# Two weight subtractions put behind the first norm factor in GpSimd's queue

## The reference, cut to what matters

```
o_na = neighbourhood_attention(q_na, k_na, v_na, na_rpb)
o_mla = latent_attention(c_q, c_kv, k_rope, ...)
mixed = concatenate([rms_norm(o_na, na_out_norm_g),
                     rms_norm(o_mla, mla_out_norm_g)]) @ w_out
h = h + rms_norm(mixed, mix_post_g)
```

## Time and profile before

| | us |
|---|---|
| median of 3 runs | 953.36 |
| lowest and highest run | 953.24, 953.84 |
| the profiled execution's own time | 953.24 |
| its span in the profile | 951.5 |

### The profile page before, as it was taken

How to read it: one execution, slowest core, us unless ns; L and a number is a source line. 1 busy time by engine, 2 the same in 40 slices (tenths; PEclk the granted TensorE clock), 3 DMA queues, 4 the chain that set the end, 5 groups by cost and what they waited for, 6 DMA issues and landing times.

```text
span 951.5 us, 14116 instructions
## 1 busy us (share of the span) xinstructions
PE 938.2 (99%) x4854; PEld 788.5 (83%) x4854; DVE 506.2 (53%) x843; ACT 488.9 (51%) x782; POOL 283.1 (30%) x141
## 2 busy tenths in 40 slices
PE   8999999999999999999999999999999999999997
PEld 7999977778888888888888888888889878888886
DVE  5858967755653434523744343356477764433323
ACT  5577456653455444444644454447355664544441
POOL 1000000000044444444344444654441044444442
PEclk9999999999999999999999999999999999999999
DMA  7755566345555556787665655655512345666562
GB/s 245 242 173 167 178 216 193 113 153 197 176 162 191 183 191 189 269 230 206 188 189 179 190 187 188 220 154 166 173 61 92 111 155 180 188 187 193 179 195 71
DMA packets 132773, 169.36 MB, mean 178 GB/s; under 512 B 16708, under 2 KB 88431, under 8 KB 132599
## 3 DMA queue, kind: packets, MB, share of 16 engines
q1 hardware_dynamic: 132566, 168.67, 55.9%
q10 hardware_dynamic: 160, 0.07, 0.0%
HBM read 167.61 MB, written 1.10 MB: 177 GB/s over the span
## 4 chain that ended last, share of the span: by engine, by line
PE 95%; DVE 2%; ACT 2%; issue 1%; POOL 0%; DVEq 0%; POOLq 0%; ACTq 0%
PE acc L852 26%; PE acc L854 25%; PE acc L853 25%; PE tp L928 4%; PE acc L910 3%; PE acc L914 3%; PE acc L912 3%; PE acc L1194 1%; PE sc L1153 1%; PE sc L1003 1%; PE tp L1022 1%; DVE w_lo L1269 1%; ACT w_hi L506 0%; ACT junk L518 0%; PE sc L946 0%
## 5 line engine op out<-in xcount | busy, mean ns | idle before, releaser
L506 ACT ACTIVATE w_hi<-w_raw 128x1024 fp32r<-128x1024 f32 x301 | 318.3, 1059 | 363.9 <-PE acc L854 318.7
L1896 POOL TENSOR_TENSOR w_lo<-w_raw,w_hi 128x1024 fp32r<-128x1024 f32 x106 | 257.1, 2425 | 554.8 <-ACT w_hi L506 554.8
L1269 DVE TENSOR_TENSOR w_lo<-w_raw,w_hi 128x1024 fp32r<-128x1024 f32 x195 | 247.6, 1273 | 278.7 <-ACT w_hi L506 278.0
L852 PE MATMUL acc<-w_hi,xt_hi 128*128 128x512 f32 x704 | 279.7, 397 | 0.6 <-DVE w_lo L1269 0.3
L854 PE MATMUL acc<-w_lo,xt_hi 128*128 128x512 f32 x704 | 274.5, 390 | 0.0
L853 PE MATMUL acc<-w_hi,xt_lo 128*128 128x512 f32 x704 | 274.1, 389 | 0.0
L852 PEld LDWEIGHTS acc<-w_hi,xt_hi 128*128 128x128 f32 x704 | 132.2, 188 | 30.9 <-issue 4.5
L854 PEld LDWEIGHTS acc<-w_lo,xt_hi 128*128 128x128 f32 x704 | 132.1, 188 | 28.1
L853 PEld LDWEIGHTS acc<-w_hi,xt_lo 128*128 128x128 f32 x704 | 132.4, 188 | 25.6
L852 PE MATMUL acc<-w_hi,hid_hi 128*128 128x512 f32 x264 | 103.4, 392 | 0.0
L854 PE MATMUL acc<-w_lo,hid_hi 128*128 128x512 f32 x264 | 102.8, 389 | 0.0
(11 more groups left out here) (208 smaller groups left out, 908.3 us busy)
## 6 DMA issues: line engine op xcount, KB each, us to landing
w_raw<-in_ffn_w_gu SPq DMA_DIRECT2D x172, 256.0 KB
w_raw<-in_w_in SPq DMA_DIRECT2D x68, 512.0 KB
w_raw<-in_w_ffn_in SPq DMA_DIRECT2D x88, 256.0 KB
w_raw<-in_ffn_w_down SPq DMA_DIRECT2D x44, 512.0 KB
w_raw<-in_w_ffn_out SPq DMA_DIRECT2D x22, 512.0 KB
w_raw<-in_w_rnn_out SPq DMA_DIRECT2D x8, 512.0 KB
w_raw<-in_w_attn_out SPq DMA_DIRECT2D x8, 512.0 KB
w_raw<-in_w_o SPq DMA_DIRECT2D x8, 512.0 KB
```

Source lines behind the costliest of these rows:

```text
L506: act.activation(w_hi[:, b, :], w_raw[:, b, :], ACT.Copy).then_inc(hi_done[b], 1)
L852: pe.matmul(o, hi[:, k, rows], wh, start=first and n == 0, stop=False)
L1269: dve.tensor_tensor(w_lo[:, b, :], w_raw[:, b, :], w_hi[:, b, :].bitcast(F32), ALU.subtract).then_inc(lo_done[b], 1)
L1896: pool.tensor_tensor(w_lo[:, b, :], w_raw[:, b, :], w_hi[:, b, :].bitcast(F32), ALU.subtract).then_inc(lo_done[b], 1)
```

## The change

GpSimd's `feed(out2, 4)` is cut in two. The subtractions of `out2` and `out2+1` stay where they are, those of `out2+2` and `out2+3` stand behind `rstd("na")`. No instruction is added or removed, and no other engine's order is changed.

```diff
@@ -1958,8 +1958,9 @@
             pool.wait_ge(pool_step, 4)
             pool.tensor_tensor(q1, rope[:, 0], rope[:, 1], ALU.subtract).then_inc(rope_q, 1)
             pool.tensor_tensor(q2, rope[:, 2], rope[:, 3], ALU.add).then_inc(rope_q, 1)
-            feed(S["out2"], 4)
+            feed(S["out2"], 2)
             rstd("na")
+            feed(S["out2"] + 2, 2)
             rstd("mla")
             rstd("mix", 0)
             rstd("mix", 1)
```

## The result

| | before | after |
|---|---|---|
| median of 14 runs, us | 953.72 | 959.22 |
| lowest and highest, us | 953.24, 954.80 | 955.80, 962.60 |
| ratio, 95% interval | | 1.0051 [1.0039, 1.0063] |

The change made the kernel slower by 5.5 us; 2.3 were forecast, with a range up to 956.2. The spread says more than the median. With each execution the mean granted clock of TensorE is recorded. Of the 41 executions of the changed kernel for which it is, 12 took 955.8 to 956.9 us at a mean clock of 0.997 to 0.999, and 29 took 958.6 to 962.6 us at 0.990 to 0.994. So there are two outcomes, and the forecast of 955.6 fits one of them. Three of the 29 took 962.5 to 962.6 us, at 0.990; no trace shows what they had more. The profiled execution is one of the slower kind, 959.65 us.

The account below looks back on a forecast made before the run. TensorE, busy 938.2 of 951.5 us (99%), was taken as the bound. Profiled 953.24 + 0 (norm factor) + 0 (loads) + 2.3 (L1825) = 955.5 us, predicted median 955.6, range 953.2 to 956.2.

Parts of the forecast that it names:

- an earlier norm factor: At rstd("na") on GpSimd: rs already starts as early as VectorE's mean square allows, so gain 0.
- a relieved 711 to 716 us: Where the two subtractions were: TensorE fully busy, VectorE's copy not slowed, gain 0; rival that it helps, 953.2 us, chance 0.02.
- Late slabs and loads hidden: Subtractions of out2+2, out2+3 and SP's loads behind them: done before their readers, some 3 us cover for loads, cost 0.
- L1825 held up by both subtractions in turn: VectorE's pair scaling the na result at 727.22: alternates with GpSimd's two subtractions, second instruction ends 3.42 us later.
- What reaches TensorE: At the ona0 transposes and step 14: after 1.31 us slack, TensorE is 2.3 us late, with a gap of 2.1 us.
- The step through the second bank: VectorE's copy of step 13 stands behind L1825, so step 14's transposes start 2.40 us late.
- the wait of 0.82 us before `ona1`: TensorE's existing wait before the ona1 transposes: not shortened, because its chain shifts whole, so it absorbs no lateness.
- the clock: TensorE's granted clock: full speed, 2.4 GHz, expected throughout, so no added cost from the gap.
- the clock falls for the 3 us of the loop's rest: Rival at the attention loop's end: lower clock, or out2+6 late by 1 or 2 us; 957.5 us or more, chance 0.04.
- No recovery behind the stage: Behind 735 us TensorE has only 0.31 us idle, so earlier lateness is paid in full at the end.

Follow-up runs that it names:

- the execution at full clock: Profiled execution, 955.81 us, of the kernel before with two useless GpSimd operations added behind rstd("na"); the clock stayed up.
- one and two fillers: Changed kernel plus one or two useless 128x256 matmuls before TensorE's wait for the scaled na result: 955.78 us (gap 1.10) and 955.81 us (gap 0.67).
- GpSimd only occupied: Kernel before, subtractions and loads in old places, plus two useless GpSimd tensor_tensor operations behind rstd("na"): 959.35 us, ratio 1.0062.
- with 1.52, all 5: Kernel before, plus two useless VectorE tensor_tensor operations ahead of the L1825 pair, GpSimd's order and loads untouched: 959.91 us, ratio 1.0059.

## Why the prediction was wrong, point by point

- Nothing to win from an earlier norm factor or from a relieved 711 to 716 us: right. `rs` follows `ms` at once in both kernels.
- Late slabs and loads hidden: right, shown by delaying the loads alone (953.78).
- L1825 held up by both subtractions in turn: right, read from the `ms` and `aux_lo` rows. The pair was forecast at 4.3 us and took 3.88: the first L1825 held up GpSimd less (4.84 us for both subtractions, against 4.66 with nothing beside them, so by 0.2 and not by 0.39), and the second L1825 ended 0.28 behind the second subtraction (731.66 against 731.38), not 0.39.
- What reaches TensorE: forecast 2.3 us, measured 2.03 in the execution at full clock, and 955.8 against 953.7 in the medians with one and two fillers. The step through the second bank (the copy of step 13) was there. That the wait of 0.82 us before `ona1` is not shortened is right at full clock only.
- The failed step is the clock: "At the end of the kernel TensorE is idle from 946 to 950 with a granted clock of 1.00, so I expect full speed". One stretch of one execution was taken as a bound, and it was cut off just before the clock fell. The next stretch of the same trace is this:

```profile
950.00:951.50 1.50, 0.00 (x0) 0.00 (x0) 0.00 (x0) 0.00 (x0) 0.00 (x0) 0.59 0.38 148
```

Nor does the clock hold that long each time: in the profile after, TensorE ends at 952.14, and the same kind of stretch, 952.5 to 954.5, is already at 0.97 on average. And in the stage itself the gap of 1.59 us was followed by 10 us at half clock in the profiled execution; 29 of 41 executions have the time and the mean clock that go with it. The term missed, which the prediction put at nothing, is 3.4 us (959.2 less 955.8). It was in the rivals ("the clock falls for the 3 us of the loop's rest"), with a chance of 0.04 and too short a duration: the low clock also took in the first products, to 742.8.
- No recovery behind the stage: right.

What stays open is why the clock falls in one execution with this gap and not in another: in the profiled one of the change it fell, in that of the kernel with GpSimd only occupied it did not, with the same pair of 3.88 us and the same gap of 1.59 in both. The wait of 0.82 us before `ona1` is not what set it off: in the profile after, the clock was down at 732.5, ahead of the place of that wait (`ona1` starts at 735.06). Whether the gap has to lie this close to other short waits was not tried.

## What to carry to other kernels

Before work is moved on GpSimd, list what VectorE reads and writes purely in SBUF in the new place: here each short instruction waited for one long one, once per turn, and the slack of its reader decided whether that showed. Where TensorE is 99% busy, price a new gap as the gap plus the clock; here 2 us of lateness became 5.5. In this kernel a matmul of no use made the gap harmless for the clock, but it is better not to make it: the same subtractions 2.2 us later, or one of them, cost nothing.

## What the runs showed of the hardware that was not expected

- TensorE's clock fell to half about 0.8 us after the work had come back (gap 730.1 to 731.7, fall at 732.5) and stayed low until 742.8, with TensorE 99% busy from 733 to 738 and 100% from 738 on.
- With a gap of 1.59 us in the profiled execution, 29 of 41 executions had a low mean clock (0.990 to 0.994), and 4 of 5 with GpSimd only occupied; with 1.52, all 5 (0.993 to 0.996); with 1.10, none of 11. What decides between the executions of one kernel is not shown.
- GpSimd's two subtractions and VectorE's two L1825 went through in turn, one instruction each: of the 3.88 us of the pair, 1.12 went by until the first subtraction's end (728.90), 2.48 with the second, and the rest, 0.28, is VectorE's own.
